# Two-layer attention and expert kernel: in the last group of tiles, sections of one tile beside attention, and the last pair's weights through the ring

## What is computed

```python
o_sb, o_nsa, o_moba = ...                              # three attentions over the projections of x
g = jax.nn.sigmoid(merge_g).reshape(B, S, 3, D)        # merge_g: 3072 columns of x @ w_in
mix = g[:, :, 0] * (o_sb @ w_br_sb) + g[:, :, 1] * (o_nsa @ w_br_nsa) + g[:, :, 2] * (o_moba @ w_br_moba)
x = layer_norm(DEEPNORM_ALPHA * x + mix @ w_out, ln1_g, ln1_b)
# peer_ffn, per block of 128 tokens
q = jnp.einsum('td,dhc->thc', xb, w_q)
s1 = jnp.einsum('thc,hkc->thk', q[..., :half], sub_k1); s2 = ...   # scores against two sets of 128 keys
v1, i1 = lax.top_k(s1, 8); v2, i2 = lax.top_k(s2, 8)               # then the best 8 of the 64 sums
act = jax.nn.gelu(jnp.einsum('thkd,td->thk', u_tab[idx], xb))
y = jnp.einsum('thk,thkd->td', g * act, v_tab[idx])
x = layer_norm(DEEPNORM_ALPHA * x + y, ln2_g, ln2_b)
```

## Time and profile before

| | us |
|---|---|
| median of the runs | 2807.62 (2806.18 to 2830.58, 3 runs) |
| span of the profiled execution | 2819.9 |
| PE busy | 2453.4 (87%) |
| DVE busy | 1942.6 (69%) |
| POOL busy | 1233.1 (44%) |
| phase 3 of group 3 | 2157 to 2309 |
| phase 4 of group 3 | 2309 to 2457 |
| last section | 2457 to 2563 |

### The profile page before, as it was taken

The page is one execution under the profiler, slowest core; times in us unless marked ns, Lnnn a source line. Parts: engine busy times, 40 slices in busy tenths (PEclk is TensorE's granted clock), DMA queues, the critical chain, the costliest instruction groups (busy, mean ns, idle before and its releaser), DMA issues.

```text
span 2819.9 us, 30185 instructions
## 1 busy us (share of the span) xinstructions
PE 2453.4 (87%) x10632; PEld 1484.2 (53%) x10632; DVE 1942.6 (69%) x4009; ACT 786.9 (28%) x1563; POOL 1233.1 (44%) x1028
## 2 busy tenths in 40 slices
PE   8998998998999989899988887999989999987126
PEld 4764476575445357657654465476445347644012
DVE  0122245588988875667886887587998886687875
ACT  2243222213344332321342212212445333301001
POOL 0000023354565432434553655164656352656775
PEclk9998999999989999999997998999999899999569
DMA  4323258787888776977896999787889685998998
GB/s 144 105 73 100 90 188 337 273 290 253 304 283 302 266 251 224 379 286 270 323 359 246 338 375 350 272 297 255 298 297 330 221 308 200 394 366 317 362 373 320
DMA packets 224183, 776.98 MB, mean 276 GB/s; under 512 B 23200, under 2 KB 39712, under 8 KB 219552
## 3 DMA queue, kind: packets, MB, share of 16 engines
q0 software_dynamic: 147456, 536.94, 52.1%
q1 hardware_dynamic: 73696, 227.80, 22.6%
q10 hardware_dynamic: 2880, 10.31, 0.9%
...
## 4 chain that ended last, share of the span: by engine, by line
PE 57%; DVE 15%; DMA 9%; issue 8%; POOL 7%; ACT 3%; another core or an unknown queue 0%; DVEq 0%; ACTq 0%; SPq 0%
PE ps L1056 14%; PE ps L931 7%; PE ps L900 6%; PE ps L984 6%; PE ps L1089 5%; POOL rows L840 4%; DVE x L1535 4%; DMA rows<-in_table_u,idx 4%; PE ps L886 3%; DMA rows<-in_table_v,idx 3%; PE ps L1124 3%; DVE rows L1520 2%; PE ps L1150 2%; DMA wring<-in_merge 2%; PE ps L993 2%
## 5 line engine op out<-in xcount | busy, mean ns | idle before, releaser
L840 POOL DMA_INDIRECT rows<-in_table_u,idx x462 | 565.2, 1223 | 1021.3 <-DVE idx L1643 506.7
L1056 PE MATMUL ps<-xT,wring 128*128 128x256 f32 x3072 | 768.1, 399 | 56.5 <-DMA wring<-in_merge 24.6
L840 POOL DMA_INDIRECT rows<-in_table_v,idx x434 | 526.5, 1213 | 490.5 <-DVE x L1535 362.4
L1056 PEld LDWEIGHTS ps<-xT,wring 128*128 128x128 f32 x3072 | 586.2, 197 | 245.4 <-issue 90.4
L1520 DVE CUSTOM_DVE_ANT_0 rows<-rows,x 128x1024 f32<-128x1024 f32 x462 | 555.0, 1223 | 120.0 <-DMA rows<-in_table_u,idx 114.3
L1535 DVE SCALAR_TENSOR_TENSOR x<-rows,wts,x 128x1024 f32<-128x1024 f32 x413 | 529.8, 1283 | 65.6 <-DMA rows<-in_table_v,idx 43.6
L1089 PE MATMUL ps<-KA,QA 33*128 33x512 f32 (+7 forms) x576 | 253.7, 537 | 26.5 <-DVE part_m L1777 12.9
L1389 ACT ACTIVATE scratch<-scratch,negm 128x640 f32<-128x640 f32 (+7 forms) x192 | 143.5, 747 | 475.3 <-DVE negm L1777 464.6
L900 PE MATMUL ps<-wring,G 128*128 128x512 f32 x384 | 184.8, 617 | 9.7 <-DVE G L1678 6.3
L1777 DVE CUSTOM_DVE_ANT_0 scratch<-ps,cst 128x128 f32<-128x128 f32 (+3 forms) x192 | 86.9, 454 | 143.0 <-PE ps L1089 140.3
L886 PE MATMUL ps<-oT,wring 128*128 128x256 f32 x384 | 126.0, 464 | 53.0 <-DVE G L1673 35.1
(11 more groups left out here) (209 smaller groups left out, 2951.4 us busy)
## 6 DMA issues: line engine op xcount, KB each, us to landing
wring<-in_merge SPq DMA_DIRECT2D x216, 512.0 KB
wring<-in_w_out_h SPq DMA_DIRECT2D x48, 512.0 KB
wring<-in_w_query SPq DMA_DIRECT2D x32, 512.0 KB
G<-in_w_query SPq DMA_DIRECT2D x12, 1024.0 KB, 8.5
G<-in_x SPq DMA_DIRECT2D x16, 512.0 KB, 4.6
G<-in_ln SPq DMA_DIRECT2D x8, 1024.0 KB, 6.8
G<-x_mid SPq DMA_DIRECT2D x16, 512.0 KB, 5.4
rows<-in_table_u,idx POOLq DMA_INDIRECT x462
```

The lines of the kernel that those rows point to most:

```text
L840: pool.indirect_dma_start(row_slot(n), None, tab_u if table == "u" else tab_v, bass.IndirectOffsetOnAxis(ap=idx[:, GT * (g % 2) + t, e:e + ...
L1056: mm = pe.matmul(gate_bank(p)[:, SW * n:SW * (n + 1)], w[:, lo:lo + P], xT[:, kc, SW * (p // HALF_GATES):SW * (p // HALF_GATES + 1)], star ...
```

## The change

In group 3 tiles 0 and 1 become sections of their own (`LAST_GROUP`): all 12 gates of the first half are made in phases 0 and 1, tile 0 goes from merge to route in phase 2, tile 1 in phase 3, the second half's gates follow in phases 3 and 4. Each single section loads all weights again and uses one bank; tile 0's x, ln1 rows and scores lie in the half of G that the second pair has not filled yet. The last pair stays a pair, with the same steps, but takes all its weights from the ring. In groups 0 to 2 the early pair's section is no longer cut: it lies whole in phase 3, and gates 12 to 23 in phase 4; score rows of phase 3 take its first half. The expert blocks of a single are u, v of the same tile, so gelu is finished ahead of the first v row (`own_next`). The planner's factors and `ahead` are set anew, and the scratch of `route` moves into G, which takes away two waits. Cut to its core; merges, outs, turns, queries and matches count tiles instead of pairs, and a single's merge and query matmuls have 128 columns:

```diff
-SECTIONS = [(g, s) for g in range(NG) for s in range(NS)]
 SW = ST * P
+LAST_GROUP = [(0,), (1,), (2, 3)]
+SECTIONS = [(g, tiles) for g in range(NG - 1) for tiles in ((0, 1), (2, 3))] + [(NG - 1, tiles) for tiles in LAST_GROUP]
+LAST = len(SECTIONS) - 1
...
+def home_half(sec):
+    return {"first": 1, "third": 0}.get(role(sec), gate_half(sec))
...
+    if tiles == 1:
+        return out[0] + out[1] + [("mean", s, 0, 0.0)]
...
-    first = [("tanh", 0, 0, 0.0)] + [("gate", 0, (HALF_GATES, part), 0.0) for part in range(PARTS)]
-    first += gate_steps(HALF_GATES + 1) + [("merge", 0, k, 1.5) for k in range(12)] + section_outs(0) + gate_steps(HALF_GATES + 2)
-    second = [("norm", 0, 1, 0.0)] + gate_steps(HALF_GATES + 3)
-    second += [("turn", 0, k, 1.5) for k in range(2 * ST)] + sum([query_steps(0, k) for k in range(4)], [])
-    second += [("match", 0, k, 1.2) for k in range(2 * ST)] + [("route", 0, tt, 0.5) for tt in range(ST)]
-    return first, second + sum([gate_steps(p) for p in range(HALF_GATES + 4, GATES)], [])
+    first = [("tanh", 0, 0, 0.0)] + [("merge", 0, k, 1.5) for k in range(12)] + section_outs(0)
+    first += [("norm", 0, 1, 0.0)] + [("turn", 0, k, 1.5) for k in range(2 * ST)] + sum([query_steps(0, k) for k in range(4)], [])
+    return first + [("match", 0, k, 1.2) for k in range(2 * ST)] + [("route", 0, tt, 0.5) for tt in range(ST)]
+def pair_section(s):
+    steps = [("tanh", s, 0, 0.0)] + [("merge", s, k, 0.9) for k in range(12)] + section_outs(s)
+    turn = [("turn", s, k, 1.5) for k in range(2 * ST)]
+    steps += turn[0:2] + [("norm", s, 1, 0.0)] + turn[2:4] + sum([query_steps(s, k) for k in range(4)], [])
+    return steps + [("match", s, k, 1.2) for k in range(2 * ST)] + [("route", s, tt, 0.5) for tt in range(ST)]
+def tile_section(s, begin=False):
+    steps = [("tanh", s, 0, 0.0)] if begin else []
+    steps += [("merge", s, k, 1.5) for k in range(6)] + section_outs(s, 1) + [("norm", s, 0, 0.0)]
+    steps += [("turn", s, k, 1.5) for k in range(2)] + sum([query_steps(s, k) for k in range(2)], [])
+    return steps + [("match", s, k, 1.2) for k in range(2)] + [("route", s, 0, 0.5)]
...
-    share = [0, 5, 9, 12]
+    share = [0, 5, 9, 12] if g + 1 < NG else [0, 6, 12, 12]
     for phase in range(GT + 1):
         streams = []
-        if phase < 3:
+        if phase < 3 and share[phase] < share[phase + 1]:
             streams.append((0.0, sum([gate_steps(p) for p in range(share[phase], share[phase + 1])], []), 1.0))
+        elif g + 1 < NG:
+            late = sum([gate_steps(p) for p in range(HALF_GATES, GATES)], [])
+            streams.append((0.0, early_section() if phase == 3 else late, 0.97))
+        elif phase == 2:
+            streams.append((0.0, tile_section(0, True), 0.97))
+        elif phase == 3:
+            streams.append((0.0, tile_section(1) + sum([gate_steps(p) for p in range(HALF_GATES, HALF_GATES + 4)], []), 0.97))
         else:
-            streams.append((0.0, early_section()[phase - 3], 0.95))
+            own = tile_section(2, True) if len(LAST_GROUP) == 4 else []
+            streams.append((0.0, sum([gate_steps(p) for p in range(HALF_GATES + 4, GATES)], []) + own, 0.97))
...
-            streams.append((0.0, row_steps(phase, GT * half + phase), 0.85))
+            streams.append((0.0, row_steps(phase, GT * half + phase), 0.5 if phase == 3 and g + 1 < NG else 0.85))
...
+        out += [("v", g, h) for h in range(2)] + [("a0", g, h) for h in range(2)] + [("gate", g, n) for n in GATES_FIRST]
+        out += sum([section_items(sec) for sec in sections_of(g, 0)], []) + [("gate", g, n) for n in GATES_LAST]
+    return out + sum([section_items(sec) for sec in sections_of(NG - 1, 1)], [])
+def section_items(sec):
+    out = [("br", sec, b) for b in (2, 1, 0)] + [("o", sec, n) for n in range(8)]
+    return out + [("q", sec, n) for n in range(8)] + [("k", sec)]
+GATES_FIRST, GATES_LAST = range(0, GATES), range(GATES, 2 * GATES)
...
-BLOCKS = [(sec, table, ST * s + tt) for sec, (g, s) in enumerate(SECTIONS)
-          for table, tt in (("u", 0), ("u", 1), ("v", 0), ("v", 1))]
+BLOCKS = [(sec, table, t) for sec, (g, tiles) in enumerate(SECTIONS) for table in ("u", "v") for t in tiles]
...
+            if kind == "tanh" or kind == "merge" and a == 0:
+                nxt = max(nxt, steps_needed(sec))
...
-            now += (.78 if kind in HEAD_KINDS or s < 0 else 1.12 if not late else 1.0 if g % 2 else 1.1) * pe
+                late = s >= 0
+            now += (.78 if kind in HEAD_KINDS or s < 0 else 1.12 if not late else 1.05) * pe
             if kind in ("tanh", "turn") and s < 0:
-                ahead = 1.0 if g == NG else TIGHT_AHEAD if kind == "tanh" else EXPERT_AHEAD
+                ahead = TIGHT_AHEAD if kind == "tanh" else EXPERT_AHEAD
+            if g >= NG - 1 and s >= 0 and kind in ("merge", "turn") and role(sec) in ("third", "last"):
+                ahead = 0.5 if kind == "merge" or g == NG else EXPERT_AHEAD
...
+def own_next(b):
+    return BLOCKS[b][1] == "u" and BLOCKS[b + 1] == (BLOCKS[b][0], "v", BLOCKS[b][2])
...
+            if role(sec) in ("late", "last"):
                 return bank(6 + k % 2)
-            return bank(6 if kind in ("merge", "out") else k % 2)
+            if role(sec) == "third":
+                return bank(k % 2)
+            return bank(6 if role(sec) in ("first", "second") or kind in ("merge", "out") else k % 2)
         def depth(sec, kind):
-            return 1 if SECTIONS[sec][1] == 0 and kind in ("merge", "out") else 2
-        def gate_bank(p):
-            return bank(1 if p > HALF_GATES + 3 and p % 2 == 0 else 6)
+            return 1 if role(sec) in ("first", "second") or role(sec) == "early" and kind in ("merge", "out") else 2
+        def own_bank(g):
+            return HALF_GATES if g + 1 < NG else HALF_GATES + 4
+        def gate_bank(g, p):
+            return bank(1 if p >= own_bank(g) and p % 2 == 0 else 6)
...
+                g, tiles = SECTIONS[sec]
+                if home_half(sec) != gate_half(sec):
+                    sp.wait_ge(idx_ready, GT * g + tiles[0])
+                else:
+                    sp.wait_ge(x1T_free, sec + 1)
+                for t in tiles:
+                    sp.dma_start(row_of(1, t, home_half(sec)), x_src(GT * g + t)).then_inc(resid_landed[t], 16)
...
+            def ring_section(sec):
+                for b in (2, 1, 0):
+                    load("br", sec, b)
+                if home_half(sec) == gate_half(sec):
+                    residual(sec)
+                for n in range(4):
+                    load("o", sec, n)
+                if home_half(sec) == gate_half(sec):
+                    norm_rows(sec)
+                for n in range(4, 8):
+                    load("o", sec, n)
+                for n in range(8):
+                    load("q", sec, n)
                 load("k", sec)
...
+                    if n == GATES - 4 and role(early[0]) == "first":
+                        residual(early[0])
+                        norm_rows(early[0])
                     load("gate", g, n)
-                for b in (2, 1, 0):
-                    load("br", sec, b)
-                residual(sec)
-                for n in range(4):
-                    load("o", sec, n)
-                norm_rows(sec)
-                for n in range(4, 8):
-                    load("o", sec, n)
-                for n in GATES_NEXT:
-                    load("gate", g, n)
-                for n in range(8):
-                    load("q", sec, n)
-                load("k", sec)
+                for sec in early:
+                    ring_section(sec)
                 for n in GATES_LAST:
                     if n == 2 * GATES - 8:
-                        used(("q", sec, 7))
-                        used(("k", sec))
+                        sp.wait_ge(idx_ready, GT * g + ST)
                         if g + 1 < NG:
                             head_rows(g + 1, 0)
                             head_rows(g + 1, 1)
-                    if n == 2 * GATES - 4:
-                        sp.wait_ge(idx_ready, GT * g + ST)
-                        load("oh", sec + 1, 0)
+                        elif role(late[0]) == "third":
+                            residual(late[0])
+                            norm_rows(late[0])
+                    if n == 2 * GATES - 4 and g + 1 < NG:
+                        load("oh", late[0], 0)
                     load("gate", g, n)
                 if g + 1 < NG:
                     head_rows(g + 1, 2)
                     sp.wait_ge(y_ready, TILES)
                     sp.dma_start(ln2_gb[:, :, :], ln2[layer].partition_broadcast(P)).then_inc(ln2_landed, 16)
-                for b in (2, 1, 0):
-                    load("br", sec + 1, b)
-            sp.wait_ge(oT_copied, GT * NG)
-            late_section(NS * NG - 1)
+                if g + 1 < NG:
+                    for b in (2, 1, 0):
+                        load("br", late[0], b)
```

(21 more changed lines are left out.)

312 lines of the change are left out of this document (175 added, 137 removed).

## The result

The changed kernel takes 2899.06 us (2893.26 to 2904.41, 4 runs) against 2806.9 us of the kernel before (4 runs): a ratio of 1.0321, 95% interval 1.0277 to 1.0364. I had forecast 2782 us. The runs that follow were made in five batches, each with its own runs of the kernel before, whose median was 2807 to 2838 us (2808 and 2838 in two batches on the same chip). So between batches ratios are compared, and microseconds only within a batch.

What follows compares the result with a forecast made beforehand. TensorE was taken to bound the kernel up to the last routing, the expert rows after it. Terms 3 - 50 + 12 + 9 + 3 - 10 + 4 + 3 = -26 us off 2807.6 gave 2782 us, range 2748 to 2822 (8 in 10).

Steps and rivals of the forecast that it cites:

- items 2 and 3: Last group: earlier indices end GpSimd's gaps, nearly all 41 backlogged gathers are done by the last routing; -50 us.
- rival C: Phase 4 of group 2: DMA bounds it, 9 us in place of 3, total -20, 2788 us; chance 0.12.
- Rival B: Before the last routing: VectorE can't take more rows, gain 8 instead of 50, total +16, 2824 us; chance 0.17.
- item 7: SP's queue: the ring wait at 1757 behind layer 0's last store goes, the gates' tanh stays; -10 us (-14 to 0).
- Item 1: Last group, pair into singles: two singles take 79.3 us of matmuls against 76, weights loaded twice; +3 us.
- item 5: Groups 0 to 2: tile 1's norm loses gate 15 as cover, 3 us each; +9 us (0 to +15).
- Item 4: Last group's singles: each norm chain lies open without another tile's out over it; two tiles, +12 us (0 to +16).
- Item 6: Last pair through the ring: late loads of w_out instead of side buffers; +3 us (0 to +8).
- item 8: Fuller VectorE, 41 more rows before the last routing: +4 us (0 to +20); fuller DMA in group 2 phase 4: +3.
- Rival D: Seams after the pair's routing: suffix sums wait for VectorE, 15 us at each of four, total +31, 2839 us; chance 0.11.

Runs made afterwards that it cites:

- experiment 1: Changed kernel with ScalarE copying the spread queries ahead of tanh in the four phases that begin with a tanh: 2855.73 us, ratio 1.0151.
- experiment 5: Kernel before with gate 12's parts weighted 1.72, so only the first stands ahead of the first stick-breaking matmul: 2863.07 us against 2835.79, ratio 1.0101.
- experiment 3: Changed kernel with groups 0 to 2 staged as in the kernel before; singles and ring stay in the last group: 2858.85 us, ratio 1.0154.
- experiment 8: Changed kernel with groups 0 to 2 as before, spread copies ahead of tanh, side buffers back, weight 6 on the singles' norm: 2837.82 us, ratio 1.003.
- 7: Changed kernel with groups 0 to 2 as before, spread copies ahead of tanh, last pair's side buffers back: 2856.11 us against 2838.27, ratio 1.0092.
- experiment 4: Changed kernel with the last pair's w_out half and w_query in side buffers again: 2881.83 us, ratio 1.024.
- experiment 11: Changed kernel with groups 0 to 2, spread-before-tanh copies and side buffers restored, and last group's tiles 0 and 1 paired in phase 3: 2832.72 us, 0.9985.
- Experiment 13: Kernel of experiment 11 with the last group's phase 4 stick stream beginning at 0.12 of the phase instead of 0: 2806.35 us against 2807.69, ratio 0.9994.
- Experiment 10: Kernel of experiment 8 with VectorE planned 0.5 us ahead instead of 3 after tile 1's routing, 864 rows placed instead of 876: 2868.3 us, ratio 1.0119.

## Why the prediction was wrong

**Right: the backlog (items 2 and 3) and the tail.** All but one of the 896 early rows are placed ahead of the last routing (840 before), the first gather of the last pair follows its index by 0.4 us, and the rest lasts 203 us against the 207 that -50 makes of 257. In the last group GpSimd no longer idles for an index of tiles 0 and 1, and in group 1 it does so for 48.7 us (62.3 before), as said. Nor was rival C it: phase 4 of group 2 took 128 us as summed, with the DMA share at 0.93, and TensorE waited 6.0 us for the ring in it, 4.9 before. Rival B is out: no gather of tiles 0 and 1 stood behind the last index. But tile 0's indices came at 2287, not at about 2197, and the last pair's first at 2691, well past the 2595 that the prediction gave as a sign of being wrong.

**Right in kind: item 7.** The 14 us for the ring at the head of group 3 are gone, and that stretch is 10 us below its sum, with a wait of 8.0 us for a merge's multiply in their place. Item 1, the matmuls of the singles, is not contradicted: TensorE's busy time rose by 14 us, at a lower clock.

**The step that failed: what the moved gates had covered (item 5).** I saw gate 15 as cover for the norm of tile 1 and costed its going at 3 us a group; that gate 12 covered anything, the sum left at nothing. I had read that ScalarE's tanh takes 5.51 us, and did not ask what on TensorE's queue stood over it. The weight 0.0 on gate 12 was in the code. What the runs showed in its place are four waits of 8 us with the lower clock behind them: 43 us (experiment 1), and with the sign turned 28 us on the kernel before (experiment 5). All of groups 0 to 2 staged anew cost 40 us net (experiment 3), and three of the four waits are among them; item 5 had +9.

**Sizes that were off.** Item 4, the singles' norm chain: +12 summed, 0 to +16 as bounds, 18 measured (experiment 8 against 7). Its waits are 8.7 and 9.0 us, not the 6.6 and 7.8 less 2 of cover that I took from the earlier trace rows. Item 6, the last pair through the ring: +3, with 8 as the bound; 17 measured (experiment 4). The 4.6 us that I took were the median of loads of x into G, and I had the first load of w_out issued 6 us ahead of `out`. It was issued 1.8 us ahead, behind the residual rows, and `out` waited 13.2 us for w_out. The page after (KB each, median us to landing) has the ring's loads of w_out at 7.0:

```profile
wring<-in_w_out_h SPq DMA_DIRECT2D x60, 512.0 KB, 7.0
```

**The step that would have failed even with these mended: item 8.** I priced 41 rows more on VectorE at +4, with 20 as the bound. With tanh, norm and side buffers put right, 35 or 36 more gathers ahead of the last index go with 41 to 45 us more of length ahead of it, with singles (experiment 8) as with a pair (experiment 11), and the tail gives back 42 to 44. VectorE is busy for 691 us instead of 638 in it, the 53 us that item 8 expected. I took it that TensorE would hardly feel them, VectorE being busy for only 78% of that stretch. But it is one queue in a fixed order: each row placed ahead of a multiply, a softplus or a maximum is a row that TensorE may wait for. Experiment 13 shows one such place in full. How much of the 41 to 45 us is the rows' is not shown: experiments 8 and 11 also have the sections, gates and routings in other places than before. Experiment 10, which changes rows alone, gives 0.8 us a row; at that price, an estimate, 36 rows are 29 us.

**Rival D** had the right mechanism for a part: 6.4 and 5.9 us in phase 4 of groups 1 and 2, and 14.2 in experiment 11, where I had 15 a seam. It was not what decided: experiment 8 has no wait of TensorE for VectorE in phase 4 of the last group, and the same sum.

**Readings.** Three of the prediction's readings of the earlier trace rows were off: the 394 GB/s are the 35th slice, not the 36th, the last four slices moved 317 to 373 GB/s, not 320 to 373, and TensorE is at 7 tenths in the 25th. None of them enters the sum.

**What stays open.** Tanh's 43 us and the 40 of groups 0 to 2 are not to be added, three of four waits being in both. Groups 0 to 2, the last tanh, the ring and the singles (40, 11, 17 and 35) make 103, and all undone is worth 3.4%, 94 us (experiment 11 against the result): within the noise they add up. What makes up the 41 to 45 us was not told apart further than into TensorE's busy time at a lower granted clock (14 to 21 us) and its gaps (24 to 26): which gaps are the rows' and which the new places', and why the clock is lower in phases 2 and 3 (0.89 and 0.86 in experiment 8, 0.94 and 0.92 before), is open, and so is whether another placement of the same rows would keep the tail's gain. No version here beats the kernel before by more than can be measured; the nearest is the pair of experiment 11, 0.9985.
